# Constants table of a two-layer decoder step loaded in two parts, and sums of squares partly added on VectorE

## The reference, cut to what matters

```python
def rmsnorm(x, g):
    y = xf * lax.rsqrt(jnp.mean(xf * xf, axis=-1, keepdims=True) + EPS)
h = modulate(x, norm_mix_g[i], sh1, sc1)        # rmsnorm, then scale and shift
m, S = retention_mixer(h, ...)                  # rotary needs cos and sin
x = x + g1[:, None, :] * m
h = modulate(x, norm_ffn_g[i], sh2, sc2)        # needs the mean of x*x over 1024 channels
```

## Time and profile before

| | |
|---|---|
| Median of 3 runs | 1653.17 us (1652.91 to 1655.23) |
| The profiled execution's own time | 1651.56 us |
| Its span, first to last instruction | 1649.7 us |
| TensorE busy | 1550.8 us, 94% of the span |
| VectorE, ScalarE busy | 729.5 and 372.6 us |
| HBM read and written | 361 GB/s over the span |
| Mean granted clock of TensorE | 0.984 of full |

### The profile page before, as it was taken

How to read it: one execution, slowest core, us unless ns; L and a number is a source line. 1 busy time by engine, 2 the same in 40 slices (tenths; PEclk the granted TensorE clock), 3 DMA queues, 4 the chain that set the end, 5 groups by cost and what they waited for, 6 DMA issues and landing times. The chain is left out here.

```text
span 1649.7 us, 29859 instructions
## 1 busy us (share of the span) xinstructions
PE 1550.8 (94%) x11320; PEld 1034.3 (63%) x11320; DVE 729.5 (44%) x2024; ACT 372.6 (23%) x784; POOL 96.3 (6%) x121
## 2 busy tenths in 40 slices
PE   6999989998999989999998799998999999999995
PEld 4778765776665655566565587766566565656653
DVE  3205435216464443544534335444655534454454
ACT  2003443113121111111211245431112111121112
POOL 0000110000000000000000000000000000000000
PEclk9999999999999999999999899999999999999998
DMA  9996799338999998999999683977999998999994
GB/s 365 385 371 246 293 398 369 110 120 326 370 420 421 419 419 333 387 420 420 421 419 417 204 283 130 346 295 275 421 419 420 419 413 333 420 420 420 420 420 168
DMA packets 150675, 580.36 MB, mean 352 GB/s; under 512 B 17341, under 2 KB 62561, under 8 KB 101290
## 3 DMA queue, kind: packets, MB, share of 16 engines
q1 hardware_dynamic: 134442, 535.74, 81.8%
q0 software_dynamic: 15488, 40.92, 6.4%
q10 hardware_dynamic: 640, 2.26, 0.3%
HBM read 568.22 MB, written 26.90 MB: 361 GB/s over the span
## 5 line engine op out<-in xcount | busy, mean ns | idle before, releaser
L2378 PE MATMUL ps<-ring,scratch 128*64 128x256 f32 x3840 | 427.2, 383 | 10.9 <-DMA ring<-in_moe_w_up 9.7
L2378 PEld LDWEIGHTS ps<-ring,scratch 128*64 128x64 f32 x3840 | 283.7, 138 | 141.5 <-issue 15.8
L2426 PE MATMUL ps<-ring,scratch 128*64 128x512 f32 x960 | 214.5, 597 | 0.0
L2339 PE MATMUL ps<-scratch 128*128 128x264 bf16 x1488 | 183.7, 277 | 5.1 <-issue 4.3
L696 PE MATMUL ps<-hT,ring 128*128 128x264 f32 x768 | 180.4, 389 | 1.3 <-ACT hT L379 1.3
L2767 DVE SCALAR_TENSOR_TENSOR scratch<-scratch,ps 128x256 f32<-128x256 f32 x64 | 30.8, 481 | 341.2 <-ACT scratch L2924 334.3
L2339 PEld LDWEIGHTS ps<-scratch 128*128 128x128 bf16 x1488 | 131.8, 98 | 58.2 <-issue 20.3
L696 PEld LDWEIGHTS ps<-hT,ring 128*128 128x128 f32 x768 | 146.0, 191 | 30.7 <-issue 2.5
L2426 PEld LDWEIGHTS ps<-ring,scratch 128*64 128x64 f32 x960 | 62.6, 136 | 125.6 <-issue 94.2
L2734 DVE TENSOR_TENSOR scratch<-scratch,ps 128x264 f32<-128x264 f32 x240 | 103.3, 431 | 77.3 <-PE ps L2339 77.0
L2924 ACT ACTIVATE scratch<-ps 128x256 f32<-128x256 f32 x64 | 24.6, 385 | 433.3 <-PE ps L2378 413.6
(11 more groups left out here) (401 smaller groups left out, 1385.6 us busy)
## 6 DMA issues: line engine op xcount, KB each, us to landing
ring<-in_moe_w_gate SPq DMA_DIRECT2D x128, 1024.0 KB, 16.4
ring<-in_moe_w_up SPq DMA_DIRECT2D x128, 1024.0 KB, 15.1
ring<-in_moe_w_down SPq DMA_DIRECT2D x128, 1024.0 KB, 15.9
ring<-in_ada_w SPq DMA_DIRECT2D x48, 1024.0 KB, 14.7
ring<-in_ret_w_in SPq DMA_DIRECT2D x24, 1024.0 KB, 16.7
ring<-in_state_ret SPq DMA_DIRECT2D x16, 1024.0 KB, 14.9
out_ret_sample<-ring POOLq DMA_DIRECT2D x16, 1024.0 KB, 8.9
ring<-in_gla_w_in SPq DMA_DIRECT2D x12, 1024.0 KB, 12.1
```

What stands on the lines that cost most here:

```text
L2339: mm = nc.tensor.matmul(k.ps[:, c % 2, 0:T], parts_of(p)[:, s, c * P:(c + 1) * P], slot_token[:, p, :], start=(p == 0 and s == 0), stop=(p ...
L2378: mm = nc.tensor.matmul(k.ps[lo:lo + CAP, 2 + p, j * DE:(j + 1) * DE], xg[:, p, c, lo:lo + CAP], slot(k, n, DE)[:, c, :], start=(c == 0), ...
L2426: mm = nc.tensor.matmul(k.ps[lo:lo + CAP, 6 + half, :], hid_t[:, p, m, lo:lo + CAP], slot(k, n, D)[:, m, half * 512:(half + 1) * 512], sta ...
```

## The change

The table's columns are reordered so that what the setup reads (identity, ones and small constants, 416 columns) comes first and cos, sin, decays and the rest (1817 columns) follow. The first piece is loaded where the whole table was; the second is issued behind load 9, the second of `ret_w_in`. VectorE waits for it ahead of `modulate_samples`. At both mixers' ends VectorE adds the squares of chunks 1 to 5 onto those of chunk 0, one add in each drain from chunk 2 to chunk 6, and TensorE does three partition sums (0, 6, 7) behind the last product in place of eight. The transposes of the late group and its store move one chunk later.

```diff
-for _name, _w in (("cos", T), ("sin", T), ("decay", RH * TP), ("kdec", 2 * RH), ("causal", P), ("ident", P),
-                  ("before", P), ("ones", P), ("pick", NS), ("own", 6), ("own4", 12), ("gtri", NG * NG),
-                  ("iota", NE + 1), ("valid", TT), ("row", TT)):
+for _name, _w in (("ident", P), ("before", P), ("ones", P), ("pick", NS), ("row", TT), ("valid", TT), ("own", 6),
+                  ("own4", 12), ("cos", T), ("sin", T), ("decay", RH * TP), ("kdec", 2 * RH), ("causal", P),
+                  ("gtri", NG * NG), ("iota", NE + 1)):
...
-TABW = _at
+TABW, TAB_FIRST = _at, TAB["cos"][0]
...
-        sp.dma_start(k.tab[:, :], inp["tables"]).then_inc(self.s_tab, 16)
+        sp.dma_start(k.tab[:, 0:TAB_FIRST], inp["tables"][:, 0:TAB_FIRST]).then_inc(self.s_tab, 16)
...
             first.sync(sp)
+            load_until(k, sp, loads[1] + 1)
+            sp.dma_start(k.tab[:, TAB_FIRST:TABW], inp["tables"][:, TAB_FIRST:TABW]).then_inc(first.s_more, 16)
             load_until(k, sp, groups[LATE][-1] + 1)
...
             def norm_sum(c):
                 pe.wait_ge(s_sq, c + 1)
+                if c == 0:
+                    pe.wait_ge(s_total, DC - 3)
...
                     products(LATE)
-                    for c in range(n):
-                        norm_sum(c)
+                elif n == OUT_HALF + 2:
                     transposes(LATE, late_rows, bank=LATE_BANK)
-                elif n > OUT_HALF + 1:
-                    norm_sum(n - 1)
-            norm_sum(DC - 1)
+            for c in (0, DC - 2, DC - 1):
+                norm_sum(c)
...
             store(0)
             store(1)
+            v.wait_ge(first.s_more, 16)
             v.wait_ge(s_mod, FIRST)
             first.modulate_samples(v)
...
                 v.wait_ge(s_x, n + 1)
-                if n == OUT_HALF + 1:
+                if 1 <= n - 1 < DC - 2:
+                    v.wait_ge(s_sq, n)
+                    if n > 2:
+                        v.wait_ge(s_total, n - 2)
+                    nc.vector.tensor_tensor(squares[:, 0, :], squares[:, 0, :], squares[:, n - 1, :], ALU.add)\
+                        .then_inc(s_total, 1)
+                if n == OUT_HALF + 2:
                     store(LATE, bank=LATE_BANK)
```

More of the change, by code:

```diff
@@ L337, in __init__ @@
              "vectors_transposed", "x_transposed", "cond_out", "vectors_out", "x_out"))
+        self.s_more = k.sem("setup_more_tables_loaded")
         self.s_sq, self.s_sum, self.s_ms, self.s_rt, self.s_gain, self.s_h, self.s_samples = (
@@ L653, in retention @@
         "sample_normed", "sample_transposed", "sample_gained", "sample_heads_out"))
-    s_half, s_add, s_x, s_sq = (k.sem(f"ret_{n}") for n in ("projected", "sample_add", "residual_added", "squared"))
+    s_half, s_add, s_x, s_sq, s_total = (k.sem(f"ret_{n}") for n in (
+        "projected", "sample_add", "residual_added", "squared", "squares_added"))
     s_ldb = [k.stored[f"ret_sample_state_stored{b}"] for b in range(8)]
@@ L1293, in gla @@
         "sample_normed", "sample_transposed", "sample_gained", "sample_heads_out"))
-    s_half, s_add, s_x, s_sq = (k.sem(f"gla_{n}") for n in ("projected", "sample_add", "residual_added", "squared"))
+    s_half, s_add, s_x, s_sq, s_total = (k.sem(f"gla_{n}") for n in (
+        "projected", "sample_add", "residual_added", "squared", "squares_added"))
     s_stb = [k.stored[f"gla_sample_state_stored{i}"] for i in range(4)]
@@ L1548, in _ @@
                     cond_products(k, pe, k.ps[:, 1], groups[GLA_LATE])
-                    for c in range(5):
-                        norm_sum(c)
+                elif n == 6:
                     pe.wait_ge(s_row, 2)
                     cond_transpose(k, k.ps[:, 2], cond_rows[:, 0]).then_inc(s_crt, 1)
[L1553 to L1556, removed]
+            for c in (0, DC - 2, DC - 1):
+                norm_sum(c)
         @block.vector
@@ L1746, in _ @@
                 v.wait_ge(s_x, n + 1)
-                if n == 5:
+                if 1 <= n - 1 < DC - 2:
+                    v.wait_ge(s_sq, n)
+                    if n > 2:
+                        v.wait_ge(s_total, n - 2)
+                    nc.vector.tensor_tensor(squares[:, 0, :], squares[:, 0, :], squares[:, n - 1, :], ALU.add)\
+                        .then_inc(s_total, 1)
+                if n == 6:
                     store(2, 2)
@@ L2013, in experts @@
     own4 = area(TT * 12).rearrange("p (t n) -> p t n", t=TT)
-    third_parts = k.tab[:, 0:3 * D // 2].bitcast(BF16).rearrange("p (s d) -> p s d", s=3)
+    third_parts = k.tab[:, TAB_FIRST:TAB_FIRST + 3 * D // 2].bitcast(BF16).rearrange("p (s d) -> p s d", s=3)
     assert TAB["decay"][1] >= 3 * D // 2
```

## The result

The changed kernel took 1657.74 us, median of 20 runs (1653.83 to 1660.30), against 1652.93 for 20 runs of the kernel before: ratio 1.003, 95% interval 1.0023 to 1.0036. It is slower by some 5 us, and 1657.74 lies above the predicted range of 1647 to 1655. The profiled execution took 1656.13 us, 4.6 more than the one of before, so the two traces show a difference of the same size.

A forecast was written before the change was run, and what follows sets the result against it. It took TensorE, busy for 94% of the span, as the bound. Start +3.9 and the two mixers' ends -2.8 each gave -1.7 us, from median 1653.17 to 1651.5 us; range 1647 to 1655, the forecast's own 1649.5 to 1653.2.

The forecast's parts named there:

- a shift of the first projection goes through to the end: After the first projection: neither queue has a schedule that would swallow a shift, so it reaches the program's end in full.
- Cost of the start: Program start: gains wait for the second piece, landing at 37.7 us; first projection starts at 38.8 or 38.9, +3.9 us.
- I count no difference: TensorE's clock at the first projection: low level before and after, counted as zero, bound 1.6 us either way.
- Gain at the mixers' ends: Retention's and GLA's ends: six partition sums of 0.466 us leave TensorE's stream ahead of the last product, 2.8 us each.
- the added sum covered: Behind each mixer's last product: the added sum (chunk 0) is free under a 1.4 us wait; uncovered it costs 0.47.
- the adds delay no drain: VectorE at the mixers' ends: five adds, 2.2 us each mixer, cost nothing on the path; uncovered, 0.43 us per add.
- The wait is free: Rival, start: second piece there when gains are due (31.7), start gains 2.3 us, total -7.9, 1645.3 us; chance 0.11.
- The second piece comes later than its bytes say: Rival, start: second piece has its own latency up to 5.1 us; +6.6 - 5.6 = +1.0, 1654.2 us; chance 0.13.
- The two microseconds that the prediction set against its sum: Start: a fixed part of about 2.0 us per DMA, if added, makes the start +5.9 and the time 1653.5.
- The sums were not worth anything: Rival, experts' stage: a transfer queue sets it, so the ends' 5.6 us go and +3.9 stays, 1657.1 us; chance 0.08.

The follow-up runs named there:

- padded ends with the change's table: The changed kernel plus five one-column TensorE products in each mixer's end, restoring the record count of the kernel before: 1654.39 us, ratio 1.002 to the kernel before.
- table alone: The changed kernel with both mixers' ends put back as before, keeping the split table and the wait ahead of the gains: 1657.98 us, ratio 1.004.
- ends -3.0 padded: The changed kernel with the table loaded in one piece and five one-column products added in each mixer's end: 1649.74 us, ratio 0.9982 to the kernel before.
- ends alone, unpadded: The changed kernel with the table loaded in one piece as before, no small products added: 1652.88 us, ratio 1.0003 to the kernel before.

## Why the prediction was wrong

It forecast -1.7 us; the medians show +4.8 and the trace +4.5. The step that failed is "a shift of the first projection goes through to the end": the sum ends at the mixers and has no term behind them. The runs showed two there, 1.54 us of low clock in the second experts' stage and 2.91 us at the last branch. Besides, the term of the start was too small, +3.9 against +4.58 in the trace, and the table's part costs +6.3 to +6.6 by the ratios. Step by step:

**Cost of the start: +3.9, measured +4.58.** The mechanism was right: VectorE's in-order wait held gains, modulation and projection until the piece landed. The landing was 38.5, not 37.7, because what stood ahead of it came only 1.3 us earlier (eighth `ada_w` at 30.39 against 31.66), not 2.3. Load 9 and the piece itself, issue and time to landing:

```profile
L299 SPq DMA_DIRECT2D ring<-in_ret_w_in x1: 11625/11625/11625, 15.5 to 15.5; - x1
...
DMA to landing us min/median/max: 20.8/20.8/20.8
```

```profile
L676 SPq DMA_DIRECT2D tab<-in_tables x1: 3336/3336/3336, 27.2 to 27.2; - x1
...
DMA to landing us min/median/max: 11.4/11.4/11.4
```

Load 9 landed at 36.3, where 35.4 was expected, and the piece 2.2 us behind it, close to the 2.3 of its bytes. Part of the missing microsecond is visible between 5 and 10 us, before and then after:

```profile
5.00:10.00 5.00, 1.38 (x10) 1.24 (x10) 0.89 (x6) 0.00 (x0) 0.00 (x0) 1.00 1.00 367
```

```profile
5.00:10.00 5.00, 2.42 (x11) 1.37 (x10) 1.09 (x3) 0.42 (x1) 0.00 (x0) 1.00 0.87 300
```

With the big table out of the way the transfer engines were no longer full (0.87); ten small loads stand between the table and the weights. That they are the reason is argued. The first `ada_w` landed 2.03 earlier. The rest, 0.76, was lost at the seventh load, which landed 3.3 us behind the sixth where the others are 2.6 apart. Why is open. The error was to price the advance by bytes alone.

**"I count no difference" for the clock: +1.49 in this trace.** It lies within the stated bound of 1.6, and within what executions of one and the same start differ by (14.74 to 17.31 us). So the choice of zero is neither confirmed nor refuted. In this pair of traces the 1.49 us count; how much of them is chance isn't known. (The stated range of 1649.5 to 1653.2 is a little wider than 1.6 either way, 1649.9 to 1653.1.)

**Gain at the mixers' ends: 2.8 each, measured 2.74 and 2.75.** Right, with the added sum covered and the adds (0.43 us each) hidden. That the adds delay no drain held too.

**The shift goes through: it did, up to the second experts,** if one leaves aside 1.35 us more between the rotation and retention's chunk 0 and 0.9 less between the two mixers. The prediction had the second experts' start 1.7 us early; it was 1.15 us late. In that stage 1.54 us were given back to a longer low clock, which was not in the sum.

**The term that wasn't there: the last branch, +2.91.** No step and no rival had it. It is the largest single error. The prediction counted what leaves TensorE's stream only as time and not as a change of the program's length, and the short branch of before was not looked at.

These five differences (0.7 + 1.5 + 0.1 + 1.5 + 2.9) make 6.7 us; other low stretches, which fall differently in each execution, give 0.5 back, and the trace's 6.2 is reached.

**The rivals.** "The wait is free" is refuted by the gains' own row. "The second piece comes later than its bytes say" isn't seen either: the gains were to be past 39 and were at 38.5, and the 0.8 us of lateness lie ahead of the piece, in load 9. (The two microseconds that the prediction set against its sum come from a section on GpSimd's path, while SyncE issues these loads; the 2.2 us from load 9's landing to the piece's leave no room for them.) "The sums were not worth anything" gave nearly the right time, 1657.1, but by luck: the sums were worth 5.5 us, and 4.4 us were lost again at two places that have nothing to do with the queue of the experts' weights.

**What stays open.** By medians the parts are: early wait and table +6.3 (padded ends with the change's table against without, 1.0020 - 0.9982) and +6.6 (table alone); ends -3.0 padded; long branch +3.5 (ends alone, unpadded against padded). They add up to between 6.8 and 7.1, and the whole change measures 4.8 to 5.0. The intervals of 1 to 3 us each way allow that. The table's 6.3 to 6.6 us are 1.5 to 2 more than the projection's delay in the traces; the clock behind the wait is the likely place, but not a shown one. Why shorter ends make the low clock in the second experts' stage longer wasn't settled.

## What to carry to other kernels

A wait placed on an in-order engine costs by what is queued behind it, so put it at the first use: here the same transfer, waited for one stage later, cost nothing (0.9983 against 0.9982 with the table whole). When a change shortens or lengthens an engine's program, look at its branches in both traces, those past skipped blocks above all, since the price can exceed the gain and a few tiny instructions can move it away. A gain isn't carried to the end of the program in full: look for stretches of low clock behind it. And before a stretch's clock is put down to a change, look at how much it differs between executions that have the same code there.

## What the runs showed of the hardware

- A branch of TensorE past a skipped block took 0.35 to 0.47 us or 3.35 to 3.70 us, depending on the number of instructions in the program ahead of it: long at 11300, 11308 and 11400 product records, short at 11320 and 11340.
- Within 7 us of that branch's start q8 moved two transfers of instructions in each of the six kernels with the long branch and one in each of the seven with the short one.
- With the same code and the same 1.32 us of idle time ahead, the first 64 products took 14.74 to 17.31 us in six executions, as TensorE's clock stood at its low level for none of the time or for part of it. With ten spare products (20 records) in the gap the clock was 1.00 throughout and they took 14.74.
- With 5.5 us less work at the two mixers' ends, the second experts' stage took 1.54 to 1.56 us longer up to its first activation in nine kernels of nine.
- A smaller first load did not bring the following ones earlier by all its missing bytes: 2.0 us of 2.3 for the first, 1.3 for the eighth.
